# Gate and up projections of a decoder layer's feed-forward stages by seven block products instead of eight

## The chip, the cores and the metric

The kernel runs on one NeuronCore of a Trainium2 chip. The metric is device time of one execution in microseconds (us), lower is better.

## The reference

One decoder layer for a sequence of 1024 tokens of width 1024, all in float32. The two feed-forward stages are where the change is made:

```python
def _swiglu(h, w_gu, w_down):
    a, b = jnp.split(h @ w_gu, 2, axis=-1)
    return (jax.nn.silu(a) * b) @ w_down
...
        x = x + 0.5 * _swiglu(_rmsnorm(x, ffn1_norm[l]), ffn1_w_gu[l], ffn1_w_down[l])
...
        x = x + merged @ w_out[l]

        x = x + 0.5 * _swiglu(_rmsnorm(x, ffn2_norm[l]), ffn2_w_gu[l], ffn2_w_down[l])
```

`w_gu` is 1024 by 5632 (gate and up, 2816 columns each), `w_down` 2816 by 1024. Between the two stages stands a mixing block: one projection of 1024 by 5632 columns, stick-breaking attention, dilated attention, attention into 256 memory tokens, three gated branches and an output projection.

## The kernel before

**Layout and precision.** The activations stand transposed in SBUF: `xT` holds 8 tiles of 128 channels by 1024 tokens. Every large product is made of float32 values split in two parts of the type fp32r, a high part (a copy on ScalarE) and a low part (a subtraction on VectorE), and three matmuls of the parts: high by high, high by low, low by high. A weight unit is 128 by 1024 numbers (512 KB): eight blocks of 128 by 128. SyncE loads units into two buffers `raw` in a fixed order; `split_hi` (line 643, ScalarE) copies one into a slot of `w_hi`, `split_lo` (line 1020, VectorE) subtracts into `w_lo`; there are three slots. `unit_done` counts what TensorE has finished, `split_done` what is ready for it.

**A feed-forward stage.** The 2816 hidden channels are 22 tiles of 128. A tile takes a gate unit and an up unit; each is 8 blocks of channels by 3 matmuls by 2 halves of the tokens, 48 matmuls of 128x512 (`product`, line 1590). The gate goes to PSUM pair 0, the up to pair 1. VectorE multiplies the gate by the tokens' norm factor `rB` (line 1055), ScalarE applies SiLU (685), VectorE scales the up (1062), multiplies (1080), copies the high part (1082) and subtracts the low part (1086). Two tiles make a group; its `down` (line 1675) is 2 units, 96 matmuls, in 8 output tiles `m` of 12, written alternately to PSUM pairs 2 and 3, and VectorE adds each of them to `xT` (`add_tile`, 1089 and line 1096); `down` waits for `down_added` before it writes a pair again.

**Order.** The order of each engine is written out by hand. TensorE runs gate and up of the tiles 2, 3, then the down of the tiles 0, 1, and so on; five turns of a loop hold two such groups each (`ffn`, line 1734), then the last down follows. In the first stage the tiles 0 and 1 are interleaved with the projections of the memory tokens and a small product for the position bias (`toe`). At the end of the first stage the last down is interleaved on ScalarE with `gain_hi` (665, the high part of `h`) and the squares (656), on GpSimd with the sums of squares (576), and on VectorE with `gain_lo` (1032); the projection that follows on TensorE takes `h` tile by tile. The mixing block, from about 760 to 1560 us, is written out without loops.

Of the kernel before, what the change touches and what calls it, by code (L numbers as in the profile page):

```python
# [25 lines left out]
P = 128  # L26
# [16 lines left out]
BODY = 6 * GT  # L43
# [5 lines left out]
U_LOOP1 = 8  # L49
FFN_UNITS = 3 * FT  # L50
# [5 lines left out]
UNITS = U_FFN2 + FFN_UNITS  # L56
BR = (HS * HD + 2 * HD + HX * HD) // P
# [164 lines left out]
def layer(nc, x, mem, weights, gains, head_gains, rel_bias, consts, onehot, out):  # L222
    ctx = ExitStack()
    with ctx:
# [43 lines left out]
        mT_hi = at("mT_hi", AR + 48 * K, [P, DT, MEM], F32R)  # L268
# [5 lines left out]
        a_hi = at("a_hi", AR, [P, 2 * GT, S], F32R)  # L274
        a_lo = at("a_lo", AR + 16 * K, [P, 2 * GT, S], F32R)
        silu = at("silu", AR + 32 * K, [P, 2, S])
        glu = at("glu", AR + 40 * K, [P, 2, S])
# [7 lines left out]
        pr_mem = [at(f"pr_mem{i}", AR + (4 + i) * K, [P, MEM]) for i in range(3)]  # L285
# [81 lines left out]
        x0_in, x0_turned, x0_taken, h0_hi_done = sem("x0_in"), sem("x0_turned"), sem("x0_taken"), sem("h0_hi_done")  # L367
        raw0_in, w0_hi_done = sem("raw0_in"), sem("w0_hi_done")
# [17 lines left out]
        acc_hi_done, acc_split, xq_square_hi, xq_split = (sem(n) for n in ("acc_hi_done", "acc_split", "xq_square_hi", "xq_split"))  # L386
# [4 lines left out]
        tri_ready, sb_soft, sb_hi, sb_lo = sem("tri_ready"), sem("sb_soft"), sem("sb_hi"), sem("sb_lo")  # L391
# [21 lines left out]
        early_half = sem("early_half")  # L413
# [5 lines left out]

        def at_turn(k, i, step=BODY):  # L420

            return k if i is None else step * i + k
# [115 lines left out]
        def _(sp):  # L538
# [11 lines left out]
            with sp.Fori(1, UNITS // NRAW) as i:  # L550
                for r in range(NRAW):
                    sp.wait_ge(split_done, NRAW * i + r - NRAW + 1)
                    sp.dma_start(raw[:, r, :], weights[bass.ds(NRAW * i + r, 1)].rearrange("a p n -> p (a n)")
                                 ).then_inc(raw_in[r], 16)
# [12 lines left out]
        def _(pool):  # L567
# [25 lines left out]
            def xq_square_split(q):  # L593

                pool.wait_ge(xq_square, q + 1)
                pool.wait_ge(xq_square_hi, q + 1)
                nc.gpsimd.tensor_tensor(xq_sq_lo[:, (q + 1) % 2, :], xq_sq[:, (q + 1) % 2, :], xq_sq_hi[:, (q + 1) % 2, :].bitcast(F32),
                                        ALU.subtract).then_inc(xq_split, 1)
# [43 lines left out]
        def _(act):  # L642
            def split_hi(k, i=None):

                if i is None and k >= UNITS:
                    return
                act.wait_ge(raw_in[k % NRAW], 16 * (at_turn(k // NRAW, i, BODY // NRAW) + 1))
                after(act, unit_done, at_turn(k, i) - NW + 1)
                nc.scalar.activation(w_hi[:, k % NW].rearrange("p a b -> p (a b)"), raw[:, k % NRAW, :],  # L649
                                     ACT.Copy).then_inc(hi_done, 1)  # L650
# [25 lines left out]
            def ffn_tile(k, t, i=None):  # L676

                split_hi(k + AHEAD, i)
                silu_tile(t, i)
                split_hi(k + 1 + AHEAD, i)  # L680

            def silu_tile(t, i=None):

                act.wait_ge(gate_scaled, at_turn(t, i, 2 * GT) + 1)
                nc.scalar.activation(silu[:, t % 2, :], silu[:, t % 2, :], ACT.Silu).then_inc(silu_done, 1)  # L685

            def ffn(f, u0):
                t0, u1 = FT * f, u0 + 2 * GT
                if f:
                    for q in range(GT):  # L690
                        ffn_tile(u0 + 2 * q, t0 + q)
                with act.Fori(0, (NGRP - 1) // 2) as i:
                    for half in range(2):
                        k = u1 + 3 * GT * half
                        for q in range(GT):
                            ffn_tile(k + 2 * q, t0 + GT * (1 + half) + q, i)
                        for q in range(GT):
                            split_hi(k + 2 * GT + q + AHEAD, i)
                for q in range(GT - 1):
                    split_hi(u0 + FFN_UNITS - GT + q + AHEAD)  # L700

# [62 lines left out]
            for k in range(DT):  # L764
                if k == 0:
                    act.wait_ge(raw0_in, 16)
                    nc.scalar.activation(w_hi[:, 0, 0, :], raw[:, 0, 0:P], ACT.Copy).then_inc(w0_hi_done, 1)
                    act.wait_ge(x0_taken, 1)
                    nc.scalar.activation(h_hi[:, 0, 0:512], xT[:, 0, 0:512], ACT.Copy, scale=g32[:, 0, 0:1]).then_inc(h0_hi_done, 1)
# [34 lines left out]
            silu_tile(0)  # L804
            act.dma_start(oh[:], onehot).then_inc(onehot_in, 16)
            split_hi(7)
            split_hi(8)
            silu_tile(1)
            split_hi(9)
            act.wait_ge(toe_kept, 2)  # L810
            act.dma_start(toe_row[:, :], toe[:, :]).then_inc(toe_out, 16)
            ffn(0, U_LOOP1 - 2 * GT)
# [51 lines left out]
            def xq_squares(q):  # L864
# [5 lines left out]
                nc.scalar.activation(xq_sq_hi[:, (q + 1) % 2, :], x_q[:, b - 6, cols], ACT.Square).then_inc(xq_square_hi, 1)  # L870
# [133 lines left out]
            ffn(1, U_FFN2)  # L1004
# [14 lines left out]
        def _(dve):  # L1019
            def split_lo(k, i=None):  # L1020

                if i is None and k >= UNITS:
                    return
# [74 lines left out]
            def add_down(g, k, m0=0, i=None, finish=None):  # L1098
# [4 lines left out]
                for m in range(m0, DT):  # L1103
# [3 lines left out]
                    if finish:  # L1107
                        finish(m)
# [1211 lines left out]
```

## Time and profile before

| | |
|---|---|
| median of 3 runs | 2309.69 us |
| lowest and highest | 2308.91 and 2310.46 us |
| span of the profiled execution | 2307.9 us, 25807 instructions |
| TensorE busy | 2292.0 us (99%), 10616 matmuls |
| VectorE, ScalarE, GpSimd busy | 1143.3, 619.1, 142.2 us (50%, 27%, 6%) |
| chain that ended last | 95% TensorE |
| granted TensorE clock | full in every slice |
| HBM read, written | 116.42 MB, 9.87 MB |

The span runs from the first to the last instruction of the one profiled execution; the runs' median is 1.8 us above it, which is what lies around the span and the spread of executions. Matmuls are pipelined, so that the 0.39 us of a matmul's record is not what it costs in a row of them; the distance between starts is.

### The profile page before, as it was taken

The numbers are of one execution on the slowest core, as the hardware profiler recorded it, in microseconds if no ns is written. First come the engines' busy times: TensorE is split into PE (matmuls) and PEld (weight loads), VectorE is DVE, ScalarE is ACT, GpSimd is POOL, SyncE is SP. The second block draws the span as 40 slices with busy tenths as digits, with TensorE's granted clock in tenths as the row PEclk, the third lists the DMA queues.
The fourth block names the chain that finished last, engine by engine and source line by source line (L and its number), as shares of the span: only waits on it lengthen the run. The fifth ranks groups of instructions, "written<-read, shape, count | busy, mean of one in ns | idle before, by whom it ended". The sixth has DMA issues, their size and how long they took to land.

```text
span 2307.9 us, 25807 instructions
## 1 busy us (share of the span) xinstructions
PE 2292.0 (99%) x10616; PEld 1855.9 (80%) x10616; DVE 1143.3 (50%) x1107; ACT 619.1 (27%) x795; POOL 142.2 (6%) x108
## 2 busy tenths in 40 slices
PE   8999999999999999999999999999999999999999
PEld 7888888888888777777778888888888888888887
DVE  7444443434445788778535333535434434444334
ACT  6211111111112578856442111324111111111111
POOL 3000000000000412221010000011000000000000
PEclk9999999999999999999999999999999999999999
DMA  5211111111112200011122111221111111111112
GB/s 167 74 46 55 46 36 55 48 52 46 54 45 71 110 28 19 28 46 37 37 29 65 55 55 46 73 101 46 46 55 45 47 53 45 51 40 55 45 55 73
DMA packets 47567, 125.77 MB, mean 54 GB/s; under 512 B 4301, under 2 KB 20973, under 8 KB 47248
## 3 DMA queue, kind: packets, MB, share of 16 engines
q1 hardware_dynamic: 45600, 112.61, 16.1%
q10 hardware_dynamic: 912, 10.11, 1.2%
q0 software_dynamic: 992, 2.15, 0.5%
q8 instruction: 47, 0.77, 0.1%
q14 instruction: 16, 0.13, 0.0%
HBM read 116.42 MB, written 9.87 MB: 55 GB/s over the span
## 4 chain that ended last, share of the span: by engine, by line
PE 95%; DVE 3%; ACT 1%; issue 0%; DMA 0%; POOL 0%; SPq 0%; another core or an unknown queue 0%; ACTq 0%; DVEq 0%
PE ps L1588 94%; DVE h_lo L1032 1%; PE ps L2130 0%; DMA x_nat<-in_x 0%; PE ps L2065 0%; DVE h_lo L1514 0%; PE ps L2222 0%; PE ps L1836 0%; DVE xT L1096 0%; ACT sb_l L844 0%; POOL sb_l L589 0%; DVE sp_lo L1310 0%; PE ps L1989 0%; ACT sb_l L842 0%; DVE w_lo L1025 0%
## 5 line engine op out<-in xcount | busy, mean ns | idle before, releaser
L1588 PE MATMUL ps<-h_hi,w_hi 128*128 128x512 f32 x2240 | 871.6, 394 | 1.6 <-ACT h_hi L771 1.0
L1588 PE MATMUL ps<-h_lo,w_hi 128*128 128x512 f32 x2240 | 861.9, 390 | 0.6 <-DVE h_lo L1514 0.4
L1588 PE MATMUL ps<-h_hi,w_lo 128*128 128x512 f32 x2240 | 699.5, 390 | 0.0
L1588 PEld LDWEIGHTS ps<-h_hi,w_hi 128*128 128x128 f32 x2240 | 420.2, 188 | 102.2 <-issue 16.6
L1588 PEld LDWEIGHTS ps<-h_hi,w_lo 128*128 128x128 f32 x2240 | 420.6, 188 | 88.5
L1588 PEld LDWEIGHTS ps<-h_lo,w_hi 128*128 128x128 f32 x2240 | 420.4, 188 | 86.1 <-DVE h_lo L1514 1.6
L649 ACT ACTIVATE w_hi<-raw 128x1024 fp32r<-128x1024 f32 x195 | 203.3, 1052 | 793.5 <-PE ps L1588 774.4
L1025 DVE TENSOR_TENSOR w_lo<-raw,w_hi 128x1024 fp32r<-128x1024 f32 x196 | 249.4, 1280 | 157.9 <-ACT w_hi L649 147.2
L1096 DVE TENSOR_TENSOR xT<-xT,ps 128x1024 f32<-128x1024 f32 x175 | 213.2, 1218 | 175.1 <-PE ps L1588 174.8
L1588 PE MATMUL ps<-a_hi,w_hi 128*128 128x512 f32 x704 | 275.0, 391 | 0.4 <-DVE xT L1096 0.4
L1588 PE MATMUL ps<-a_lo,w_hi 128*128 128x512 f32 x704 | 273.9, 389 | 0.0
L1588 PE MATMUL ps<-a_hi,w_lo 128*128 128x512 f32 x704 | 217.1, 389 | 0.0
L1062 DVE SCALAR_TENSOR_TENSOR glu<-ps,rB 128x1024 f32<-128x1024 f32 x44 | 53.9, 1224 | 265.1 <-PE ps L1588 265.1
L1055 DVE TENSOR_TENSOR silu<-ps,rB 128x1024 f32<-128x1024 f32 x44 | 53.8, 1224 | 252.1 <-PE ps L1588 252.1
L685 ACT ACTIVATE silu<-silu 128x1024 f32<-128x1024 f32 x44 | 46.6, 1060 | 439.6 <-DVE silu L1055 439.6
L1588 PEld LDWEIGHTS ps<-a_hi,w_hi 128*128 128x128 f32 x704 | 132.1, 188 | 29.0 <-DVE xT L1096 1.9
L1588 PEld LDWEIGHTS ps<-a_hi,w_lo 128*128 128x128 f32 x704 | 132.1, 188 | 27.6
L1588 PEld LDWEIGHTS ps<-a_lo,w_hi 128*128 128x128 f32 x704 | 132.2, 188 | 27.1
L576 POOL TENSOR_TENSOR acc<-acc,sq 128x1024 f32<-128x1024 f32 x21 | 56.1, 2673 | 1080.6 <-ACT sq L656 1079.9
L1454 DVE TENSOR_TENSOR gate<-ps,rB 128x1024 f32<-128x1024 f32 x24 | 29.4, 1224 | 130.3 <-PE ps L1588 130.3
L955 ACT ACTIVATE gate<-gate 128x1024 f32<-128x1024 f32 x24 | 25.0, 1057 | 172.7 <-DVE gate L1454 172.6
L1080 DVE TENSOR_TENSOR glu<-glu,silu 128x1024 f32<-128x1024 f32 x44 | 53.9, 1225 | 4.4
(236 smaller groups left out, 1578.8 us busy)
## 6 DMA issues: line engine op xcount, KB each, us to landing
raw<-in_weights SPq DMA_DIRECT2D x195, 512.0 KB, 3.6
x_keep<-xT ACTq DMA_DIRECT2D x1, 4096.0 KB, 12.4
x_back<-x_keep ACTq DMA_DIRECT2D x1, 4096.0 KB, 13.4
x_nat<-in_x SPq DMA_DIRECT2D x7, 512.0 KB, 7.5
out<-y_nat SPq DMA_DIRECT2D x7, 512.0 KB, 3.2
toe_keep<-toe_row ACTq DMA_DIRECT2D x2, 704.0 KB, 6.5
m_nat<-in_mem SPq DMA_DIRECT2D x1, 1024.0 KB, 8.1
d_fB<-d_f_keep POOLq DMA_DIRECT2D x2, 512.0 KB, 6.8
```

Of the source, the lines that this page charges most:

```text
L576: nc.gpsimd.tensor_tensor(acc[:], acc[:], sq[:, k % 2, :], ALU.add).then_inc(acc_done, 1)
L649: nc.scalar.activation(w_hi[:, k % NW].rearrange("p a b -> p (a b)"), raw[:, k % NRAW, :], ACT.Copy).then_inc(hi_done, 1)
L685: nc.scalar.activation(silu[:, t % 2, :], silu[:, t % 2, :], ACT.Silu).then_inc(silu_done, 1)
L955: nc.scalar.activation(gate_tile(m, b), gate_tile(m, b), ACT.Sigmoid).then_inc(gate_done, 1)
L1025: nc.vector.tensor_tensor(w_lo[:, k % NW].rearrange("p a b -> p (a b)"), raw[:, k % NRAW, :], w_hi[:, k % NW].rearrange("p a b -> p (a b)" ...
L1032: nc.vector.scalar_tensor_tensor(out=h_lo[:, k, :], in0=xT[:, k, :], scalar=g32[:, gain, k:k + 1], in1=h_hi[:, k, :].bitcast(F32), op0=ALU ...
L1055: nc.vector.tensor_tensor(silu[:, t % 2, :], ps[:, 0, :], rB[:], ALU.mult).then_inc(gate_scaled, 1)
L1062: nc.vector.scalar_tensor_tensor(out=glu[:, t % 2, :], in0=ps[:, 1, :], scalar=0.5, in1=rB[:], op0=ALU.mult, op1=ALU.mult).then_inc(up_sca ...
L1080: nc.vector.tensor_tensor(glu[:, t % 2, :], glu[:, t % 2, :], silu[:, t % 2, :], ALU.mult).then_inc(glu_done, 1)
L1096: nc.vector.tensor_tensor(xT[:, m, :], xT[:, m, :], ps[:, 2 + m % 2, :], ALU.add).then_inc(down_added, 1)
L1454: nc.vector.tensor_tensor(gate_tile(m, b), ps[:, merge_pair(m, b), :], rB[:], ALU.mult).then_inc(mg_taken, 1)
L1588: return pe.matmul(o, a, b, start=start, stop=stop, skip_group_check=True)
```

## The change

It computes 18 of the 22 tiles of each stage in another way and writes both stages out without loops.

The operands of a tile are seen as blocks: the weights as 2 by 2 (gate or up, by channels 0 to 511 or 512 to 1023), the tokens' `h` as 2 by 2 (the same halves of the channels, by tokens 0 to 511 or 512 to 1023). Strassen's scheme (in Winograd's form) makes the 2 by 2 result of seven block products. A block product is 4 blocks of channels by 3 matmuls of 128x512, 12 matmuls, and sums of its operands and results are made on VectorE, ScalarE and in PSUM:

- `quadrant`, `tokens_again`, `tokens_sum` (VectorE) make once for each stage four quadrants of `h`, norm factor included, and four differences of them, eight operands in all; `tokens_hi` (ScalarE) and `tokens_lo` (VectorE) split each, 128x2048 numbers an instruction.
- `weights_sum` (VectorE) makes four sums of weight blocks for a tile, `part_hi` and `part_lo` split the seven left operands, 128x512 each, into a ring of four buffers `q_hi` and `q_lo` that takes the place of `w_hi` and `w_lo`.
- `seventh` (TensorE) runs one of the seven products, `part_done` counts them. `behind_part` copies three partial results out of PSUM on ScalarE (`seven_kept`), adds to them on VectorE (`seven_added`), and does SiLU, product and split for half of the tokens at a time.
- The down products of the groups 1 to 10 go in four parts of 24 matmuls through the same ring (`down_part`). Order: tile 4, down 1, tile 5, tile 6, down 2, ..., tile 20, down 9, tile 21, down 10.
- The tiles 0 to 3 stay plain; for the tiles 2 and 3 `by_halves` reads the quadrants in place of `h`, and down 0 stands between the two halves of tile 2's gate.
- SyncE loads the weights of the 28 chunks (18 tiles, 10 downs) of a stage as 1 MB transfers.
- Around them: at the end of the first stage `split_hi(U_SB)`, the first weights of the mixing block, stands behind the second square on ScalarE, since the ring occupies the slots until then; slots are given by `w_slot`; some semaphores of other parts are merged.

```diff
+PLAIN, SEVEN, NQ = 4, 7, 4
+TILES7 = FT - PLAIN
...
+CHUNK = []
+for _t in range(PLAIN, FT):
+    CHUNK += [("tile", _t)]
+    CHUNK += [("down", (_t - 2) // 2)] if _t % 2 == 0 else []
+CHUNK += [("down", NGRP - 1)]
...
+            def chunks(f):
+
+                for c in range(CHUNKS):
+                    if c == 0:
+                        sp.wait_ge(split_done, U_HALVES[f] + 6)
+                    elif c == 1:
+                        sp.wait_ge(unit_done, U_HALVES[f] + 6)
+                    else:
+                        sp.wait_ge(part_split, NPART * f + chunk_end(c - 2))
...
+                elif p == 1:
+                    nc.scalar.activation(a_up[s][:, T1], bank(3), ACT.Copy).then_inc(seven_kept, 1)
...
+                for n in range(NPART):
+                    if n:
+                        behind_part(f, n - 1)
+                    if n == 0:
+                        tokens_hi(f, 6)
+                    if n + 3 < NPART:
+                        part_hi(f, n + 3)
+                    if n == 0:
+                        halves_hi(f, 3)
+                    if n == 1:
+                        tokens_hi(f, 7)
...
                 act.wait_ge(down_added, DT * (NGRP - 1) + k + 1)
                 gain_hi(k, 1)
                 square(1, k)
+                if k == 1:
+                    split_hi(U_SB)
...
+            def weights_sum(f, n, p):
...
+                if p == 1:
+                    nc.vector.tensor_tensor(to, a21, a22, ALU.add).then_inc(w_summed, 1)
...
+                if p == 3:
+                    nc.vector.tensor_tensor(a_full[s][:, T1], a_full[s][:, T1], bank(3), ALU.add).then_inc(seven_added, 1)
+                elif p == 4:
+                    nc.vector.tensor_tensor(a_up[s][:, T1], a_up[s][:, T1], bank(t % 2), ALU.add).then_inc(seven_added, 1)
...
+                    nc.vector.scalar_tensor_tensor(out=a_full[s][:, T1], in0=a_up[s][:, T1], scalar=0.5, in1=a_full[s][:, T1],
+                                                   op0=ALU.mult, op1=ALU.mult).then_inc(glu_done, 1)
...
+            def seventh(f, n):
+
+                kind, t, p, c = PARTS[n]
+                i = TILES7 * f + t - PLAIN
+                to, of = (bank(2) if p == 5 else bank(3) if p in (1, 3) else bank(t % 2)), (1, 4, 5, 3, 6, 0, 7)[p]
...
+                elif p in (2, 3, 4):
+                    pe.wait_ge(seven_kept, 3 * i + p - 1)
...
+                for j in range(4):
+                    hi, lo = (w[n % NQ][:, j * P:(j + 1) * P] for w in (q_hi, q_lo))
+                    mm(to, hi, tok_hi[of][:, j, :], j == 0 and p in (0, 1, 5), False)
+                    mm(to, hi, tok_lo[of][:, j, :], False, False)
+                    last = mm(to, lo, tok_hi[of][:, j, :], False, j == 3)
+                last.then_inc(part_done, 1)
```

How the instructions of VectorE stand in the order, first for the work of one tile. Before, inside the loop (`silu` and `glu` are the gate and the up of a tile):

```order
L1055 TENSOR_TENSOR silu<-ps,rB 128x1024
L1024 REGISTER_ALU
L1025 TENSOR_TENSOR w_lo<-raw,w_hi 128x1024
L1060 REGISTER_ALU
L1062 SCALAR_TENSOR_TENSOR glu<-ps,rB 128x1024
L1078 REGISTER_ALU
L1080 TENSOR_TENSOR glu<-glu,silu 128x1024
L1082 CAST a_hi<-glu 128x1024
L1086 TENSOR_TENSOR a_lo<-glu,a_hi 128x1024
L1024 REGISTER_ALU
L1025 TENSOR_TENSOR w_lo<-raw,w_hi 128x1024
```

Now, behind the fourth product of a tile, up to the down products' additions (`a_up` and `a_full` hold up and gate, `q_lo` are low parts of the ring):

```order
L1390 TENSOR_TENSOR a_full_71<-a_full_71,ps 128x512
L1371 TENSOR_TENSOR q_lo_114<-raw_0_107,q_hi_110 128x512
L1392 TENSOR_TENSOR a_up_77<-a_up_77,ps 128x512
L1395 SCALAR_TENSOR_TENSOR a_full_71<-a_up_77,a_full_71 128x512
L1363 TENSOR_TENSOR q_lo_115<-raw_1_108,q_hi_111 128x512
L1398 TENSOR_TENSOR a_full_71<-a_full_71,ps 128x512
L1363 TENSOR_TENSOR q_lo_116<-raw_1_108,q_hi_112 128x512
L1401 SCALAR_TENSOR_TENSOR a_full_71<-ps,a_full_71 128x512
L1409 TENSOR_TENSOR a_lo_74<-a_full_71,a_hi_80 128x512
L1363 TENSOR_TENSOR q_lo_113<-raw_1_108,q_hi_109 128x512
L1409 TENSOR_TENSOR a_lo_74<-a_full_71,a_hi_80 128x512
L1314 TENSOR_TENSOR xT<-xT,ps 128x1024 x2
```

Fewer wide instructions have become many of half the width: 18 of 128x512 for one tile (the four sums of weights and some low parts stand ahead of these rows), where four of 128x1024, a cast and the splits of two units stood.

The second place is the end of the first stage on ScalarE, behind the last part of the last down (`acc` and `sq` are squares, `h_hi` the high part of `h`). Before:

```order
L649 ACTIVATE w_hi<-raw 128x1024
L813 ACT_TABLE_LOAD
L816 DMA toe_keep<-toe_row 128x1408 x2
L665 ACTIVATE h_hi<-xT,g_58 128x1024
L656 ACTIVATE acc<-xT 128x1024
L665 ACTIVATE h_hi<-xT,g_58 128x1024
```

Now:

```order
L1006 ACT_TABLE_LOAD
L1009 DMA toe_keep<-toe_row 128x1408 x2
L778 ACTIVATE h_hi<-xT,g_58 128x1024
L769 ACTIVATE acc<-xT 128x1024
L778 ACTIVATE h_hi<-xT,g_58 128x1024
L769 ACTIVATE sq<-xT 128x1024
L762 ACTIVATE w_hi<-raw 128x1024
```

The split `w_hi` of the mixing block's first weights, which stood ahead of the first `h_hi` before, is now behind the second square. On VectorE the matching `w_lo` stands now, as before, ahead of the third addition to `xT`:

```order
L1314 TENSOR_TENSOR xT<-xT,ps 128x1024 x2
L1237 SCALAR_TENSOR_TENSOR h_lo<-xT,g_58,h_hi 128x1024
L1363 TENSOR_TENSOR q_lo_114<-raw_1_108,q_hi_110 128x512
L1230 TENSOR_TENSOR w_lo<-raw,w_hi 128x1024
L1314 TENSOR_TENSOR xT<-xT,ps 128x1024
```

## Rows read from the trace of the kernel before

**Rows 1.** The page: busy time of the engines, granted clock, the chain that ended last.
```profile
PE 2292.0 (99%) x10616; PEld 1855.9 (80%) x10616; DVE 1143.3 (50%) x1107; ACT 619.1 (27%) x795; POOL 142.2 (6%) x108
...
PEclk9999999999999999999999999999999999999999
...
PE 95%; DVE 3%; ACT 1%; issue 0%; DMA 0%; POOL 0%; SPq 0%; another core or an unknown queue 0%; ACTq 0%; DVEq 0%
```

**Rows 2.** What TensorE waited for: total us, times, longest us.
```profile
PE ps L1842 <- DMA x_nat<-in_x: 4.1, 1, 4.1
PE ps L1588 <- DVE sb_a L1317: 1.2, 5, 0.3
```

**Rows 3.** VectorE in time order, second stage's loop: start us, duration us, instruction.
```profile
1893.24 1.23 DVE L1055 TENSOR_TENSOR silu<-ps,rB 128x1024 f32<-128x1024 f32 x1 [7.49 <-PE ps L1588]
...
1958.42 1.23 DVE L1055 TENSOR_TENSOR silu<-ps,rB 128x1024 f32<-128x1024 f32 x1 [7.39 <-PE ps L1588]
...
2023.80 1.22 DVE L1055 TENSOR_TENSOR silu<-ps,rB 128x1024 f32<-128x1024 f32 x1 [7.48 <-PE ps L1588]
```

**Rows 4.** VectorE in time order, mixing block, written out: gate units' results.
```profile
1357.76 1.22 DVE L1454 TENSOR_TENSOR gate<-ps,rB 128x1024 f32<-128x1024 f32 x1 [6.36 <-PE ps L1588]
1376.80 1.23 DVE L1454 TENSOR_TENSOR gate<-ps,rB 128x1024 f32<-128x1024 f32 x1 [6.16 <-PE ps L1588]
1387.68 1.22 DVE L1454 TENSOR_TENSOR gate<-ps,rB 128x1024 f32<-128x1024 f32 x1 [6.36 <-PE ps L1588]
```

**Rows 5.** Single lines: durations in ns (least, median, most), first and last start.
```profile
L1344 DVE TENSOR_TENSOR sb_qk<-pr_x,sb_qk x8: 680/682/685, 812.6 to 915.3; 128x512 fp32r<-128x512 f32 x8
...
L1338 DVE TENSOR_TENSOR pr_x<-ps,rB x10: 690/692/693, 829.2 to 1001.8; 128x512 f32<-128x512 f32 x10
...
L1096 DVE TENSOR_TENSOR xT<-xT,ps x175: 1206/1220/1223, 128.3 to 2298.9; 128x1024 f32<-128x1024 f32 x175
...
L870 ACT ACTIVATE xq_sq_hi<-x_q x4: 617/620/623, 947.3 to 984.4; 128x512 fp32r<-128x512 f32 x4
...
L649 ACT ACTIVATE w_hi<-raw x195: 1040/1045/1065, 10.4 to 2273.9; 128x1024 fp32r<-128x1024 f32 x195
```

**Rows 6.** Windows of the loops: length, busy us of PE, PEld, DVE, ACT, POOL, clock.
```profile
80.00:740.00 660.00, 660.00 (x2911) 545.15 (x2908) 283.92 (x248) 83.89 (x83) 0.00 (x0) 1.00 0.16 49
```

**Rows 7.** The page: DMA issues, KB each, us from issue to landing.
```profile
raw<-in_weights SPq DMA_DIRECT2D x195, 512.0 KB, 3.6
...
m_nat<-in_mem SPq DMA_DIRECT2D x1, 1024.0 KB, 8.1
```

**Rows 8.** VectorE in time order, beginning of the first stage.
```profile
60.52 0.43 DVE L1172 SCALAR_TENSOR_TENSOR pr_mem<-ps,pr_mem 128x256 f32<-128x256 f32 x1 [3.97 <-ACT pr_mem L743]
...
72.03 0.42 DVE L1183 COPY mv<-ps 128x256 f32<-128x256 f32 x1 [1.25 <-PE ps L1827]
78.88 1.22 DVE L1062 SCALAR_TENSOR_TENSOR glu<-ps,rB 128x1024 f32<-128x1024 f32 x1 [6.43 <-PE ps L1588]
81.34 1.21 DVE L1267 COPY toe<-ps 2x1024 f32<-2x1024 f32 x1 [1.24 <-PE ps L1588]
```

**Rows 9.** End of the first stage in time order: ScalarE, VectorE, TensorE, GpSimd.
```profile
743.01 1.04 ACT L656 ACTIVATE sq<-xT 128x1024 f32<-128x1024 f32 x1
...
742.40 1.22 DVE L1025 TENSOR_TENSOR w_lo<-raw,w_hi 128x1024 fp32r<-128x1024 f32 x1
743.54 1.21 DVE L1096 TENSOR_TENSOR xT<-xT,ps 128x1024 f32<-128x1024 f32 x1
...
747.83 0.61 PE L1588 MATMUL ps<-a_hi,w_lo 128*128 128x512 f32 x2
748.81 0.50 PE L1588 MATMUL ps<-a_hi,w_hi 128*128 128x512 f32 x1 [0.37 <-DVE xT L1096]
...
744.14 2.41 POOL L576 TENSOR_TENSOR acc<-acc,sq 128x1024 f32<-128x1024 f32 x1 [704.16 <-ACT sq L656]
```

**Rows 10.** VectorE in time order beside a busy GpSimd.
```profile
1558.25 2.57 DVE L1025 TENSOR_TENSOR w_lo<-raw,w_hi 128x1024 fp32r<-128x1024 f32 x1 [2.07 <-ACT w_hi L649]
```

More of the change, by code:

```diff
@@ L412, in layer @@
         y_turned, y_ready, y_out = sem("y_turned"), sem("y_ready"), sem("y_out")
-        early_half = sem("early_half")
+        tok_made, tok_hi_done, tok_split = (sem(f"tok_{n}") for n in ("made", "hi_done", "split"))
+        w_summed, part_hi_done, part_split, part_done = (sem(n) for n in ("w_summed", "part_hi_done", "part_split", "part_done"))
+        seven_kept, seven_added = sem("seven_kept"), sem("seven_added")
         def after(eng, s, value):
@@ L674, in rstd, with silu_tile @@
                 nc.scalar.activation(sq[:, 0, :], rB[:], ACT.Square).then_inc(rstd_done, 1)
[L676 to L700, printed above, removed]
+            def silu_tile(f, t):
+                act.wait_ge(gate_scaled, 2 * f + t + 1)
+                nc.scalar.activation(a_full[t][:], a_full[t][:], ACT.Silu).then_inc(silu_done, 1)
@@ new lines, in glu_product, with quadrant @@
+                nc.vector.tensor_tensor(a_lo[t][:], a_full[t][:], a_hi[t][:].bitcast(F32), ALU.subtract).then_inc(a_ready, 1)
+            def quadrant(f, to, half_d, half_t, j0=0, j1=4):
+                for j in range(j0, j1):
+                    k = 4 * half_d + j
+                    nc.vector.scalar_tensor_tensor(out=tok[to][:, j, :], in0=xT[:, k, BOTH[half_t]], scalar=g32[:, 2 * f, k:k + 1],
+                                                   in1=rB[:, BOTH[half_t]], op0=ALU.mult, op1=ALU.mult).then_inc(tok_made, 1)
@@ new lines, in by_halves @@
+            def by_halves(f, part, k, half):
+                for half_d in (1, 0):
+                    i = ((1, 0), (2, 3))[half][half_d]
+                    pe.wait_ge(tok_split, 8 * f + i + 1)
+                    for j in range(4):
+                        hi, lo = (w[:, w_slot(k), 4 * half_d + j, :] for w in (w_hi, w_lo))
+                        mm(bank(2 * part + half), hi, tok_hi[i][:, j, :], half_d == 1 and j == 0, False)
+                        mm(bank(2 * part + half), hi, tok_lo[i][:, j, :], False, False)
+                        last = mm(bank(2 * part + half), lo, tok_hi[i][:, j, :], False, half_d == 0 and j == 3)
+                return last
@@ new lines, in down_mm @@
+            def down_mm(m, q, hi, lo, t, first, final, halves=BOTH, within=None):
+                for cols in halves:
+                    if within and cols == T1:
+                        within()
+                    mm(ps[:, 2 + m % 2, cols], hi, a_hi[t % 3][:, cols], first, False)
+                    mm(ps[:, 2 + m % 2, cols], hi, a_lo[t % 3][:, cols], False, False)
+                for cols in halves:
+                    last = mm(ps[:, 2 + m % 2, cols], lo, a_hi[t % 3][:, cols], False, final)
+                return last
@@ L2288, in weight_units @@
         units += gates[m] + [branches[m]]
[L2289 removed]
+    plain, chunks = swiglu_units(f2_gu, f2_down)
+    units += column_units(w_out, range(DT)) + plain + chunks
     return np.ascontiguousarray(np.stack(units))
```

694 lines of the change are left out of this document (485 added, 209 removed).

## The prediction, made before the run

> **What bounds the kernel now.** I read the page first: TensorE is busy 99% of the span, the chain that ended last is 95% TensorE, and the granted clock is full in every slice (2.4 GHz, the higher of its two levels) [rows 1]. Then its waits: the largest is the first load of x, 4.1 us once, and the next entry is 1.2 us in five pieces [rows 2]. So time goes down only by fewer or cheaper matmuls, and goes up by any new wait of TensorE. For the price of a matmul I do not take its record of 0.39 us, since the records overlap, but the distance of equal places in the loop: from the first to the third result of a group's first gate it is 2023.80 - 1893.24 = 130.56 us [rows 3], two groups of 288 matmuls, so 0.2267 us each. The single groups take 65.18 and 65.38 us, one with the loop's end and one without; together they are exactly 576 matmuls, so the turn of the loop costs nothing that shows, and writing the loops out gains nothing.
>
> **The matmuls.** Before, a tile takes 2 x 48 = 96 matmuls of 128x512, after it 7 x 12 = 84. The type (fp32r), the width and the weight load for each matmul stay. 18 tiles x 2 stages x 12 = 432 matmuls go, and the down products and tiles 0 to 3 keep theirs. 432 x 0.2267 = **97.9 us less**.
> The row says 0.2267 us, with a weight load for each matmul. The Trainium skill has another figure: "TensorE: Matmul & The Clock Gate", section "Back-to-back issue gap", gives about 131 ns as the sustained spacing at width 512 in a stream of loads and matmuls; by it the gain would be 432 x 0.131 = 57 us. The trace contradicts it, and the row decides.
>
> **The boundaries.** Each product now begins behind three semaphore waits, and there are 252 product boundaries and 80 of down parts in both stages. The nearest rows are in the mixing block, which is written out as well: from 1376.80 to 1387.68 one gate unit of 48 matmuls, 10.88 us, and from 1357.76 to 1376.80 three branch products and a gate unit, 84 matmuls behind four product boundaries with one to three waits, 19.04 us [rows 4]. Both are 0.2267 us a matmul, so a wait that is already granted costs nothing. I take 0 for each boundary. A wait that is granted late costs what it is late and about 0.2 us more: from the pair at 747.83 to the next matmul it is 0.98 us in place of 0.45, 0.53 more for a wait of 0.37 [rows 9].
>
> **VectorE in the steady state.** Per tile it makes 4 sums of weights, 7 low parts, 3 additions, 2 products and 2 low parts of the result, 18 instructions of 128x512 as the order counts them; per down 4 low parts of that width and 8 additions of 128x1024. The 512-wide ones take 0.68 us from SBUF and 0.69 from PSUM, the additions 1.22 [rows 5]. A group is then 40 x 0.69 + 8 x 1.22 = 37.4 us of VectorE in 264 x 0.2267 = 59.8 us of TensorE, 62% against 43% before [rows 6]. ScalarE: 7 high parts, 3 copies, 2 SiLU, 2 high parts of the result per tile, 4 per down, 32 x 0.62 = 19.8 us [rows 5]. A product lasts 12 x 0.2267 = 2.72 us, and the tightest handoff gives one product's time: the product p1 ends, ScalarE copies it out (0.6 us) during p2, and p3 writes over it. A ring entry is split by VectorE after the product three ahead of it began and needs at most 0.69 + 0.69 + 0.68 us of queue before it, with 5.4 us to go. Both fit. Transfers: 1 MB landed in 8.1 us, beside others, and 512 KB in 3.6 [rows 7]; a chunk is asked for when the one two before it is split, seven products or 19 us ahead. **Cost 0.**
> A rule speaks against this part: the Trainium skill, "Advanced Engine Details and Errata", section "The Read-Write Bubble", tells to use large tiles, since each instruction of VectorE and ScalarE exposes the memory's latency. The rows bear the size out (two of 512 take 1.38 us, one of 1024 1.22), and halving the width thus adds 40 x 0.08 = 3.2 us to a group, inside VectorE's free 22 us.
>
> **The start of each stage.** Eight operands have to be made of the tokens. No row is 2048 wide; from 0.69 at 512 and 1.22 at 1024 [rows 5] I extrapolate 2.28 us, back to back 2.2, and for ScalarE 1.9. In the first stage VectorE sits idle for 3.97 us before 60.52, which takes the first quadrant (4 x 0.64 = 2.6 us), and idles again between 72.5 and 78.88 [rows 8], which takes a low part, the second quadrant and a weight split. Its second low part ends about 81.7, the scaling of the up slips from 78.88 to 81.7, and the low part of tile 1 is ready near 89.0. TensorE, which ends the small product at 81.3, then has 24 matmuls by halves (to 86.6) and 12 of down 0 (to 89.4): no wait. But then VectorE makes the third quadrant before it adds the first output tile, at 92.7, which output tile 2 wants at 92.1: 0.7 + 0.2, **0.9 us**. In the second stage no small product is in the way and this falls within 0.1 us. In both, when the plain tiles end, ScalarE has the seventh split of the tokens, two high parts, tile 3's high part, the copy of p0, and the last split of the tokens (2 us) queued ahead of the copy of p1, and so ends that copy 8.7 us after the plain tiles' end, where p3 wants it after 3 x 2.72 = 8.2: 0.6 + 0.2, **0.8 us in each, 1.6**. Bounds for the start together: 0 (the extrapolated widths are too long) and 7 us (VectorE 1 us later at each of the four places in each stage).
>
> **The end of the first stage.** Here a step is moved. Before, VectorE split the next weights at 742.40 and added output tile 2 at 743.54, done at 744.75, ahead of the 745.4 at which TensorE wanted its pair [rows 9]. Now the high part comes behind the second square, which ended at 744.05; it takes 1.05, so the low part starts at 745.1, and GpSimd's first sum starts at 744.14 as well. Alone the low part takes 1.2 us, beside GpSimd it took 2.57 [rows 10]. Tile 2 is added at 747.5 to 748.9: TensorE waits 2.1 to 3.5, I take the middle and 0.2 for the late wait, 3.0. The last tile's low part comes about 0.3 us late for the last down. Before had the late wait of 0.5 us there [rows 9], which these replace. Net **2.8 us** (2.1 to 3.5). In the second stage's end the split is not there: 0.
>
> **Sum.** 2307.9 - 97.9 + 0.9 + 1.6 + 2.8 = 2215.3 us of span. The median of the runs stands 1.8 above the span shown, so 2217.1, rounded to **2217 us**. About 0.2% (4.6 us) is what a measurement of this kernel can tell from no change.
>
> **The rivals.**
> *Late handoffs in every tile* (0.13). The chain PSUM, ScalarE copy, VectorE addition, SiLU, product has to keep up with 2.72 us. For it: four-deep ring, strict order on two engines, three waits per product. Against: 62% and 33% load. Once in a tile, 0.2 for a late wait and 0.4 lateness: 36 x 0.6 = 22 us, 2239.
> *Boundaries cost after all* (0.05). If each of the 332 took 0.11 us, half of what a late wait adds: 37 us, 2253. Against it stand the two distances in the mixing block [rows 4].
> *VectorE becomes the bound, slower than before* (0.03). It decides once 40 x d + 8 x 1.22 exceeds 59.8 us, d = 1.25 us for a 512-wide instruction; before's 65.3 us for a group is passed at d = 1.39. The only row near is the 2.57 us of a 1024-wide one beside GpSimd [rows 10], 1.29 for half. Such slow instructions with a per-instruction rest, 1.5 us each, would make a group 69.8 us; with 9 groups in each of two stages that is 10.0 us more than forecast, 18 x 10.0 = 180 us, 2397. Against it: GpSimd is idle from 80 to 740 us [rows 6] and the change gives it nothing there.
> *The granted clock falls* (0.01). Short waits of TensorE in every product could let it fall to 1.2 GHz; then the two stages' 36 x 19 = 684 us of products would double, far above before, near 2900. Against: the clock stays full in the mixing block, where TensorE waits most [rows 1]. The Trainium skill, "TensorE: Matmul & The Clock Gate", section "A second HAM failure mode: psum-queue depth-cycling", describes such a fall from small idles between matmul groups; no row here shows it.
> *The change does not save what it says*: the order shows 432 fewer matmuls, the loop's turns counted, so only their price could differ.
>
> **How the numbers follow.** The forecast has 0.78; its own range goes by the bounds: with the start at 0 and the end at 2.1 the sum gives 2213.9, and 4 us less for the spread of executions and for small waits of before that go, 2210; with the start at 7 and the end at 3.5 it gives 2222.3, and 4 us more for as many late waits again that I overlook, 2226. The range that should hold 8 of 10 reaches to the first rival: 2210 to 2240. Faster by over 0.2%: 0.78 + 0.13 + 0.05 = 0.96, taken as 0.95; slower 0.04; within 0.2%: 0.01.
>
> **What would show it.** Right: TensorE's starts of equal products of two tiles 59.8 us a group apart; VectorE near 60% busy there; 10184 matmuls; waits of TensorE on lines of the two stages of some 5 us in sum, the longest near the end of the first on an addition to xT. Wrong: a wait on `seven_kept`, `part_split` or `seven_added` repeated 36 times; 512-wide instructions above 0.8 us; a clock below full in the loops' place.

## The result, and the profile after the change

The changed kernel takes **2219.24 us** in the median, the kernel before beside it 2310.07; the ratio is 0.9605, with a 95% interval of 0.959 to 0.962. Measured a second time (e11) it takes 2217.30 (2216.93 to 2220.80), ratio 0.9604. The forecast was 2217, the range 2210 to 2240. One execution here took 9163.63 us and one in e5 4972.23, for no reason that was found; the two medians on record count them, the ratios do not, and without them the medians are 2218.72 here and 2214.94 in e5. Where a difference from the changed kernel is given below, it is from **2218.0 us**, the median of its other eight executions in both measurements (2216.93 to 2220.80).

The page of the changed kernel, the lines that answer to [rows 1]:

```profile
span 2215.4 us, 25422 instructions
...
PE 2196.4 (99%) x10184; PEld 1775.5 (80%) x10184; DVE 1354.8 (61%) x1591; ACT 844.4 (38%) x1251; POOL 139.8 (6%) x108
...
PEclk9999999999999999999999999999999999999999
...
PE 96%; DVE 2%; ACT 1%; issue 1%; DMA 0%; POOL 0%; SPq 0%; ACTq 0%; DVEq 0%
```

TensorE is still at 99% and still the chain; only its work is less. The engine that filled up is VectorE, and its windows say how far: length, busy time of PE, PEld, DVE, ACT and POOL, granted clock, between equal places of two groups and over most of the first stage (before: [rows 6]):

```profile
319.22:379.03 59.81, 59.81 (x265) 49.53 (x264) 35.52 (x48) 18.81 (x32) 0.00 (x0) 1.00 0.15 54
120.00:680.00 560.00, 559.61 (x2469) 463.08 (x2469) 338.28 (x439) 178.14 (x293) 0.00 (x0) 1.00 0.15 53
```

What TensorE waited for (before: [rows 2]), the entries that are new or grew. Two lines of the stages are among them, the addition to xT and an "issue":

```profile
PE ps L1931 <- DVE xT L1314: 3.1, 1, 3.1
PE ps L1931 <- issue: 0.8, 2, 0.4
```

**The end of the first stage**, in time order, answers to [rows 9]. VectorE:

```profile
697.05 2.49 DVE L1230 TENSOR_TENSOR w_lo<-raw,w_hi 128x1024 fp32r<-128x1024 f32 x1 [2.02 <-ACT w_hi L762]
699.46 1.21 DVE L1314 TENSOR_TENSOR xT<-xT,ps 128x1024 f32<-128x1024 f32 x1
```

TensorE there, and the window that belongs to it:

```profile
700.82 0.76 PE L1931 MATMUL ps<-a_hi,q_hi 128*128 128x512 f32 x1 [3.07 <-DVE xT L1314]
701.38 0.63 PE L1931 MATMUL ps<-a_lo,q_hi 128*128 128x512 f32 x1
701.81 0.63 PE L1931 MATMUL ps<-a_hi,q_hi 128*128 128x512 f32 x1
702.23 0.63 PE L1931 MATMUL ps<-a_lo,q_hi 128*128 128x512 f32 x1
702.66 1.05 PE L1931 MATMUL ps<-a_hi,q_lo 128*128 128x512 f32 x2
703.51 0.48 PE L1931 MATMUL ps<-a_hi,q_hi 128*128 128x512 f32 x1
```

```profile
700.80:703.50 2.70, 2.68 (x6) 2.13 (x7) 2.20 (x2) 2.47 (x3) 0.62 (x1) 0.50 0.45 170
```

The predicted chain is there link by link: the high part of the next weights comes behind the second square, VectorE waits 2.02 us for it, its low part takes 2.49 us while GpSimd works, and only then is output tile 2 added, 3.07 us late. Behind the wait stands something that was not predicted: matmuls start 0.43 us apart in place of 0.23, at a granted clock of 0.50, the lower of its two levels (1.2 GHz). The page's line of the clock, 55 us to a digit, does not show it; the window does.

### The profile page after: what moved, and what is told of

Its sections match the earlier page's. It is cut to its first block, busy times and chain, and to the rows that moved or that the text cites. A ratio compares the mean times of both kernels' runs of the same rounds, so it can differ in the third digit from the quotient of the medians.

```text
span 2215.4 us, 25422 instructions
## 1 busy us (share of the span) xinstructions
PE 2196.4 (99%) x10184; PEld 1775.5 (80%) x10184; DVE 1354.8 (61%) x1591; ACT 844.4 (38%) x1251; POOL 139.8 (6%) x108
## 4 chain that ended last, share of the span: by engine, by line
PE 96%; DVE 2%; ACT 1%; issue 1%; DMA 0%; POOL 0%; SPq 0%; ACTq 0%; DVEq 0%
PE ps L1931 94%; PE ps L2527 1%; DMA x_nat<-in_x 0%; PE ps L2462 0%; DVE h_lo L1843 0%; PE ps L2619 0%; PE ps L2234 0%; DVE w_lo L1230 0%; ACT w_hi L762 0%; ACT sb_l L1039 0%; POOL sb_l L698 0%; DVE sp_lo L1639 0%; PE ps L2386 0%; ACT sb_l L1037 0%; DVE sb_a L1646 0%
## 5 line engine op out<-in xcount | busy, mean ns | idle before, releaser
L1931 PE MATMUL ps<-tok_hi,q_hi 128*128 128x512 f32 x1008 | 392.3, 389 | 0.8 <-issue 0.8
L1931 PE MATMUL ps<-tok_hi,q_lo 128*128 128x512 f32 x1008 | 392.1, 389 | 0.0
L1931 PE MATMUL ps<-tok_lo,q_hi 128*128 128x512 f32 x1008 | 392.1, 389 | 0.0
L1931 PE MATMUL ps<-h_hi,w_hi 128*128 128x512 f32 x960 | 373.4, 400 | 1.7 <-ACT h_hi L962 1.1
L1931 PE MATMUL ps<-h_lo,w_hi 128*128 128x512 f32 x960 | 363.8, 391 | 0.6 <-DVE h_lo L1843 0.6
L1931 PE MATMUL ps<-h_hi,w_lo 128*128 128x512 f32 x960 | 305.5, 390 | 0.0
L1931 PE MATMUL ps<-a_hi,q_hi 128*128 128x512 f32 x640 | 250.7, 392 | 3.1 <-DVE xT L1314 3.1
L1931 PE MATMUL ps<-a_lo,q_hi 128*128 128x512 f32 x640 | 249.5, 390 | 0.0
L1931 PEld LDWEIGHTS ps<-h_hi,w_lo 128*128 128x128 f32 x960 | 180.3, 188 | 38.7
L1931 PEld LDWEIGHTS ps<-h_lo,w_hi 128*128 128x128 f32 x960 | 180.1, 188 | 36.0 <-DVE h_lo L1843 1.7
```

The source lines that it names most:

```text
L1931: return pe.matmul(o, a, b, start=start, stop=stop, skip_group_check=True)
```

## The experiments

**Is the time all TensorE's?** e1 gives back the removed product, e2 multiplies the waits, e10 leaves out a further product's worth of each tile, so that its output is no longer the layer's. All three edit the loop of `seventh`.

```diff
-                for j in range(4):
+                for j in (range(4) if p else (0, 1, 2, 3, 0, 1, 2, 3)):     # e1
+                    pe.wait_ge(part_split, NPART * f + n + 1)               # e2, inside the old loop
+                for j in ((0, 3) if p in (2, 4) else range(4)):             # e10
```

> The first of the seven products of every tile is computed twice, the second pass starting its sum anew: 96 matmuls per tile as before the change, with every other instruction, wait and the missing loops of the changed kernel. Theory (TensorE alone sets the time, one matmul is 0.2267 us, everything else the change added lies beside it but for some 5 us at the ends): 36 x 12 x 0.2267 = 97.9 us more than the changed kernel, 2219.2 + 97.9 = 2317.1, that is 7 above the kernel before. Rival (the products wait in each tile on a handoff, which longer first products would cover): part of the added work is hidden, below 2310. Rival (a matmul of this stream costs less than 0.2267, with another loss of the same size beside it): the rise is below 90 us.

Measured: 2315.22 us (2312.93 to 2316.01), ratio to before 1.0024 (1.0014 to 1.0033). 97.2 us more than the changed kernel, where 97.9 was expected, and 6.0 above the kernel before. Both rivals fall for the tiles at large: nothing repeated in every tile was waiting. On a small scale the first holds at the start of the stages, for the two waits of 0.40 and 0.39 us of the changed kernel's trace (at p3, the fourth product of a tile; see e6) are gone, covered by the longer first product. In their place this trace has a wait of 1.68 us on the mixing block's weights, which comes up again in e11.

> Every product of a tile waits before each of its four steps of three matmuls once more on the semaphore of its weights, which is already granted: 4 x 252 = 1008 waits more in both stages. Theory (a granted wait costs nothing on TensorE): 2219, within 1 us of the changed kernel. Rival (a boundary costs about 0.11 us even if granted): 1008 x 0.11 = 111 us more, 2330; at 0.02 us each it would still be 20 us more.

Measured: 2217.51 us, ratio 0.9602 (0.9586 to 0.9618). That is 0.5 us less than the changed kernel, inside its scatter: 1008 waits cost nothing that shows, and at 0.02 us each they would have cost 20. The run prices waits that are already granted. That a boundary as a whole is free is shown by the distance of two groups, 59.84 us for 264 matmuls with all their boundaries, 0.2267 us each.

> Left out: the middle two of the four steps of the third and the fifth product of every tile, 12 matmuls, so that a tile has 72; every other instruction and wait stays. It asks whether TensorE would still be the bound of one saving more of the same size. Theory (TensorE alone sets the time, VectorE's load goes from 60 to 66%): 97.9 us less than the changed kernel, 2121, or up to 10 more where a shortened product of 1.36 us makes the handoff behind it late. Rival (the handoffs have no more to give): above 2150.

Measured: 2123.83 us, ratio 0.9197 (0.9183 to 0.9211), 94.2 less than the changed kernel. Equal additions of two tiles a group apart, in e10:

```profile
322.84 0.69 DVE L1390 TENSOR_TENSOR a_full<-a_full,ps 128x512 f32<-128x512 f32 x1 [2.24 <-PE ps L1931]
...
377.24 0.69 DVE L1390 TENSOR_TENSOR a_full<-a_full,ps 128x512 f32<-128x512 f32 x1 [2.24 <-PE ps L1931]
```

54.40 us = 240 x 0.2267: the steady state would give the whole of one saving more. Of the 97.9 us 3.7 are missing. Some 2.7 of them are at the start of the stages, where p3's wait grew from 0.40 to 1.75 us, twice, and 1 is a longer wait on `d_st` in the mixing block (1.9 in place of 0.8).

**How much room does VectorE have?** The repeats go in front of the four sums of weights and of the low parts of p0, p5 and p6; `N` is 1 in e9, 2 in e3, 3 in e4.

```diff
+            def more(*args):
+                for _ in range(N):
+                    nc.vector.tensor_tensor(*args).then_inc(again, 1)
+                    repeats[0] += 1
+                    dve.wait_ge(again, repeats[0])
...
+                    more(to, a21, a22, ALU.add)
                     nc.vector.tensor_tensor(to, a21, a22, ALU.add).then_inc(w_summed, 1)
```

> Seven 512-wide instructions of VectorE per tile (the four sums of weights and the low parts of the three unsummed weights) are each made three times, each repeat waiting for the one before it. VectorE's load is 36.1 us of a group's 59.8 now; 28 instructions of 0.69 more give 55.4 to 58.2 us, 93 to 97%. Theory (VectorE has slack and its handoffs have several us of queue): little change in the mean but some late handoffs where the repeats lie in bursts, 0 to 1 us a tile, 2219 to 2255. Rival (the handoffs are tight already, each late one costs its whole lateness): a product stretched by the repeats in front of the additions, 1.4 us a tile and more, above 2270.

> The same seven instructions four times. VectorE's load is 36.1 + 42 x 0.69 = 65.1 us a group without the time between a repeat and its wait, 69.3 with 0.1 us for each. Theory (VectorE becomes the bound when its load passes 59.8 us a group): a group takes 65.1 to 69.3, 18 groups x (5.3 to 9.5) = 95 to 171 us more, 2314 to 2390, and TensorE waits in every tile. Rival (something else sets the pace of the group, VectorE's work is hidden behind it): below 2280.

> The same seven instructions of VectorE per tile twice. Three times cost 5.3 us a group of 59.8 (65.1 between equal waits), 28 instructions more; four times cost 8.0 us more for the next 14, 0.57 each. Theory (a hinge: below some load nothing is late, above it each further instruction counts in full; 5.3 / 0.57 = 9 of the 28 are beyond it): 14 more lie inside the slack, 2219 to 2225. Rival (each added instruction costs from the first one on, 0.19 us): 18 x 14 x 0.19 = 48 us, 2267.

Measured: twice 2223.85 us (2223.26 to 2224.34), three times 2313.32 (2311.58 to 2315.55), four times 2452.95 (2447.70 to 2453.65). Twice came out as its theory said, within 2219 to 2225. Three times was expected within 2219 to 2255 by the theory, and came out with its rival. Four times was expected at 2314 to 2390 and lies 63 us above that, so the rule behind it, that VectorE binds once its load passes the 59.8 us of TensorE's work, is wrong too: it binds earlier. The windows of e3 and e4:

```profile
120.00:680.00 560.00, 526.81 (x2267) 423.38 (x2266) 468.74 (x638) 160.46 (x269) 0.00 (x0) 1.00 0.14 49
```

```profile
120.00:680.00 560.00, 491.68 (x2020) 390.31 (x2020) 487.57 (x672) 143.80 (x241) 0.00 (x0) 0.96 0.12 43
```

VectorE sets the pace at 84% busy (468.74 of 560), and reaches only 87% when pressed further. In e4 part of the time is TensorE's clock, 0.96 in this window. TensorE's waits in one group of e3, all there are between equal places 65.10 us apart:

```profile
319.09 0.47 PE L1945 MATMUL ps<-a_hi,q_hi 128*128 128x512 f32 x1 [1.21 <-DVE xT L1315]
344.06 0.50 PE L1945 MATMUL ps<-tok_hi,q_hi 128*128 128x512 f32 x1 [0.25 <-DVE q_lo L1385]
347.51 0.50 PE L1945 MATMUL ps<-tok_hi,q_hi 128*128 128x512 f32 x1 [0.43 <-DVE q_lo L1385]
352.05 0.47 PE L1945 MATMUL ps<-tok_hi,q_hi 128*128 128x512 f32 x1 [1.51 <-DVE q_lo L1385]
355.50 0.47 PE L1945 MATMUL ps<-tok_hi,q_hi 128*128 128x512 f32 x1 [0.45 <-issue]
384.19 0.47 PE L1945 MATMUL ps<-a_hi,q_hi 128*128 128x512 f32 x1 [1.21 <-DVE xT L1315]
```

Five late waits in a group, 3.85 us, and what a late wait adds each time; 18 x (65.10 - 59.84) = 94.7 us, measured 95.3. And while it set the pace VectorE still stood idle, over two groups 9.8 us ahead of additions, for results of TensorE (its group of that line, busy us, mean ns, idle us before):

```profile
L1315 DVE TENSOR_TENSOR xT<-xT,ps 128x1024 f32<-128x1024 f32 x16 | 19.3, 1218 | 9.8 <-PE ps L1945 9.8
```

In these two groups VectorE was idle for 21.6 us, 16.5 of them ahead of instructions that take a result of TensorE. It works through a written order, so it stops at a result that is not there yet, and splits that TensorE will want stand queued behind; the two engines wait for each other in turn, and neither is full. The 84% belongs to this order and to repeats that stand in bursts, each behind a wait for the one before it; no run spreads them out. With everything twice a group takes 60.03 us (equal additions at 321.18 and 381.21), 0.19 more than without, 3.4 us in the kernel. The rest of the 5.8 us is at the starts, where p3 waits 1.84 and 1.85 us in place of 0.40 and 0.39. So 14 instructions more are nearly free, the next 14 cost 5.07 us a group, 0.36 each, and the 14 after them 7.8, 0.55 each.

**The two places that were predicted to wait.** Both get their own edit (e5, e6), e7 has both, e8 moves the other end of the same handoff.

```diff
-                        if f == 0 and n == NPART - 3:    # VectorE, ffn: split_lo(U_SB)
+                        if f == 0 and n == NPART - 2:    # e5, e7
...
-                    if n == 1:                           # ScalarE, ffn: tokens_hi(f, 7)
+                    if n == 2:                           # e6, e7
...
-                if k == 1:                               # ScalarE, behind ffn(0): split_hi(U_SB)
+                if k == 0:                               # e8
```

> At the end of the first stage VectorE splits the next stage's first weights one part later, behind the addition of output tile 3 in place of ahead of that of output tile 2. Theory (the wait of 3.07 us is the queue in front of that addition, and the half clock behind it, some 1.3 us, is its consequence): the wait goes down to 0.4 us or less, no slice there shows the clock at half, and the kernel is 3.5 to 4.5 us faster than the changed one, 2214.7 to 2215.7. Rival (the half clock comes from elsewhere, e.g. the change of stage): only 2.5 to 3.0 us, and matmuls 0.43 us apart stay near 700 us. Rival (the split is late next and the projection behind the stage waits for it): less than 1 us.

Measured: 2214.94 us (2215.21 on record, see the result), ratio 0.9593 (0.9580 to 0.9605). That is 3.1 us less, under the 3.5 to 4.5 expected, and the time alone does not tell the theory from its first rival; but its five executions (2214.76 to 2215.57) all lie below the changed kernel's eight, and the trace decides for the theory. The wait has gone and the clock stays full where the matmuls had been 0.43 us apart. In its place three short waits of 0.3 to 0.4 us stand on later additions; with some 0.2 us for each late wait they take back 1.7 of the 4.6 us lost there (worked out in the next section), which fits the 3.1:

```profile
PE ps L1931 <- DVE xT L1314: 1.1, 3, 0.4
```

```profile
700.80:702.60 1.80, 1.50 (x7) 1.11 (x7) 1.80 (x2) 1.35 (x2) 1.54 (x1) 1.00 0.00 0
```

> ScalarE makes the high part of the next stage's first weights after the first square in place of the second; VectorE's order stays. The high part then starts at 693.9 in place of 695.9, VectorE's low part at about 695.0, alone 1.2 us long, and output tile 2 is added at 696.2 to 697.4, ahead of the 697.75 at which TensorE wants its pair; but output tile 1's high part and square come 1 us later each. Theory (wait is only the queue): TensorE's wait of 3.07 us goes to 0.3 or less and the clock stays full, 3.3 to 4.4 us faster than the changed kernel. Rival (GpSimd's sum or the later squares slow what follows): a gain of 1 to 2 us.

Measured: 2215.59 us, ratio 0.9595 (0.9582 to 0.9607), 2.4 us less, between the 3.3 to 4.4 of the theory and the 1 to 2 of its rival. Half of each holds. Output tile 2 is added 2.1 us earlier than in the changed kernel, not 3.3, and TensorE still waits 1.04 us for it; a second wait of 1.15 us comes in on output tile 3's addition, which stands behind a low part that runs beside GpSimd's sum, as the rival said:

```profile
698.49 3.16 DVE L1237 SCALAR_TENSOR_TENSOR h_lo<-xT,g,h_hi 128x1024 fp32r<-128x1024 f32 x1
```

```profile
698.18 2.39 POOL L685 TENSOR_TENSOR acc<-acc,sq 128x1024 f32<-128x1024 f32 x1 [658.31 <-ACT sq L769]
```

The clock stays full behind both waits.

> ScalarE makes the high part of the eighth sum of tokens after the copy of the second product and the high part of the sixth weights, not ahead of that copy. Theory (p3 waits 0.40 and 0.39 us for that copy, 0.55 us with what a late wait adds): both gaps go and nothing else becomes late, 1.1 us less in all, 2218.1. Rival (VectorE's low part of it comes later and holds back the addition of the fourth product): no gain or a loss of up to 2 us.

Measured: 2218.04 us (2215.27 to 2220.70), ratio 0.9606 (0.9593 to 0.9618). The executions scatter over 5 us and their median is that of the changed kernel's eight, so the time settles nothing. The trace does: in the changed kernel TensorE waits twice at p3,

```profile
155.74 0.47 PE L1931 MATMUL ps<-tok_hi,q_hi 128*128 128x512 f32 x1 [0.40 <-issue]
...
1650.83 0.47 PE L1931 MATMUL ps<-tok_hi,q_hi 128*128 128x512 f32 x1 [0.39 <-issue]
```

and in e6, as in e7, there is no wait from 140 to 172 us nor from 1640 to 1670.

> Both moves together. Theory (they touch different places): the gains add, 4.6 to 5.6 us less than the changed kernel, 2213.6 to 2214.6. Rival: one of them is not there.

Measured: **2213.51 us** (2213.26 to 2214.39), ratio 0.9586 (0.9574 to 0.9599): 1.4 us less than e5's 2214.94, and 4.5 less than the changed kernel, just short of the 4.6 to 5.6 expected. Its slowest execution is faster than the fastest of e5 and of the changed kernel. It is the fastest kernel of the study that computes the whole layer.

**The scatter.** The changed kernel's executions lie within 3.9 us, those of e7 within 1.1.

> The changed kernel itself, unchanged, beside the others of this call. It asks two things: whether the 3.07 us wait at the end of the first stage is there again (theory: yes, it is the order of VectorE's queue, 3.0 to 3.1 us), and whether TensorE's granted clock falls to half behind it (it did in the changed kernel's trace and not in that of the run with the later split of the tokens, with the same wait). If the clock's fall is a matter of the single execution, times scatter over 1 to 2 us around 2219, where the kernels without the wait kept within 1.1.

Measured: 2217.30 us. The wait of 3.07 us is there again, and the clock fell again. The profiled execution took 2219.41 us and has a wait that the first one did not have, on the next weights' low part. In e11 VectorE and GpSimd:

```profile
723.99 3.40 DVE L1230 TENSOR_TENSOR w_lo<-raw,w_hi 128x1024 fp32r<-128x1024 f32 x1
```

```profile
722.95 3.35 POOL L688 TENSOR_TENSOR acc_lo<-acc,acc_hi 128x1024 fp32r<-128x1024 f32 x1 [1.17 <-ACT acc_hi L774]
```

```profile
727.43 0.74 PE L1931 MATMUL ps<-h_hi,w_lo 128*128 128x512 f32 x2 [1.67 <-DVE w_lo L1230]
```

and in the first trace, 2217.16 us, with the starts the other way round:

```profile
723.56 1.21 DVE L1230 TENSOR_TENSOR w_lo<-raw,w_hi 128x1024 fp32r<-128x1024 f32 x1
```

```profile
723.73 3.30 POOL L688 TENSOR_TENSOR acc_lo<-acc,acc_hi 128x1024 fp32r<-128x1024 f32 x1 [1.18 <-ACT acc_hi L774]
```

e12 fixes that order:

```diff
                     pool.wait_ge(acc_hi_done, r)
+                    if r == 1:
+                        pool.wait_ge(split_done, U_SB + AHEAD)
```

> The changed kernel, where GpSimd's last step on the first stage's squares (acc_lo) also waits until VectorE has split the second weights of the mixing block. In the traces so far this split took 1.21 us where it began 0.16 to 0.17 us ahead of acc_lo, and 3.40 where acc_lo began 1.0 us ahead of it, and then TensorE waited 1.67 us. Theory (this order, left to chance, makes the executions of the changed kernel scatter over 3.9 us): VectorE's split takes 1.2 us, no wait on it, and the times keep within 1.5 us, median 2217. TensorE's wait of 3.07 us and the half clock behind it are not touched. Rival (the scatter comes from the clock's fall): the times still spread over 3 us or more. Price, if the order was right anyway: GpSimd starts some 1 us later, 0 to 0.5 us.

Measured: 2218.94 us (2218.61 to 2219.70), ratio 0.9606 (0.9593 to 0.9619). VectorE's split took 1.21 us and nothing waited for it; the times keep within 1.1 us in place of 3.9, though the clock still fell in the profiled one. The median did not come down to 2217.

That the order is the source of most of the scatter is not shown by this, on 5 executions against 8, for the record has a second source beside it. Each execution's mean granted clock is known: of the changed kernel's eight the fastest has 1.000, the two slowest have 0.998, the five between them 0.999, and e1's ten fall apart in the same way, three at 1.000 from 2312.93 to 2313.11 us and seven at 0.999 from 2315.01 to 2316.01. None of e12's five has 0.998. Nor are the two sources apart: the split took 3.4 us in five traces (e1, e2, e3, e4, e11), in all of which the clock had fallen at the end of the first stage, and in none of the five in which it stayed full there (e5 to e9). The fall shifts what follows and so can turn the order over. How much of the scatter each makes was not separated.

e12's trace has a new wait of 0.23 us of TensorE on acc_lo, the price named, and one of 1.3 us on `d_st` in the mixing block, which e10's has too (1.4) and the changed kernel's has not. What sets that one off was not tried.

## Why the prediction was right, step by step

- **The matmuls, -97.9 us: right.** Equal additions a group apart stand at 319.22 and 379.06, 59.84 us = 264 x 0.2267, against (65.18 + 65.38)/2 = 65.28 before. 18 x 5.44 = 97.9. e1 gives it back with 97 us and e10 takes it once more in the steady state. The other price considered, 57 us by the spacing in the Trainium skill, "TensorE: Matmul & The Clock Gate", section "Back-to-back issue gap", is contradicted by all three.
- **The boundaries, 0: right.** e2 shows it for granted waits, the 59.84 us for the boundaries as a whole. Loops written out, seven products, new waits and new order come together to e1's 6.0 us over the kernel before; e1's trace has no wait at p3, and the start's 0.3, the end's 4.1 and the 1.68 us wait on the mixing block's weights make 6.1.
- **VectorE, cost 0: right, for a reason that was too weak.** The load was overestimated a little, 37.4 us a group against 35.52: the durations of neighbours overlap, 319.22 to 319.83 for one of 0.69 us. What failed is the rival's deciding point, that VectorE becomes the bound "once 40 x d + 8 x 1.22 exceeds 59.8 us". By e3 it binds at 84% busy, 54.3 us of work in a group of 65.1. Of the "free 22 us" some 10 can be used: e9 takes 9.3 of them nearly for nothing (44.77 us busy in a group of 60.03), e3's next 9.6 cost 5. None of the signs named for the rivals is in the changed kernel's trace: no wait is repeated 36 times, the 512-wide instructions take 0.69 us, and the clock is full over the steady state.
- **The start, 0.9 and 1.6 us: places right, sizes too large.** VectorE's third quadrant took 2.73 us from 88.15, and the first addition started at 90.98; TensorE's start gaps there sum to 0.3 us in place of 0.9 (92.26 after a pair that began at 91.62, and 0.11 behind it). p3's wait was 0.40 and 0.39 us, with what a late wait adds 0.55 each, 1.1 in place of 1.6. e6 shows the named cause, the last split of the tokens ahead of the copy of p1. The upper bound of 7 us for the start names eight places at 1 us, which would be 8; nothing came near either.
- **The end, net 2.8 us: mechanism right, and one term missing.** Predicted were 3.0 for the late addition with its late wait, less the 0.5 of before. From 697.13 to 703.51 TensorE starts 8 matmuls, 8 x 0.2267 = 1.8 us of work in 6.38, so the loss is 4.6: 3.07 of wait, some 0.3 that follow a late wait, and 1.2 at half clock (five starts 0.43 us apart in place of 0.23, and a longer first one). Net 4.1. The text held a fall of the clock possible in every product and priced it there, but not behind the one long wait it forecast itself.
- **The sum.** 2307.9 - 97.9 + 0.3 + 1.1 + 4.1 = 2215.5, the span is 2215.4. That the forecast's 2215.3 comes within 0.1 us of it is luck: starts 1.1 us too high stand against an end 1.3 too low. The 1.8 us from span to time hold for each execution, but the profiled one (2217.16 us) is the second fastest of the eight; the median of the eight stands 2.6 us above its span.

## What to carry to other kernels

Where one engine is the chain at 99%, taking work from it pays by the measured distance of equal places, not by record durations, and granted waits cost nothing. The engine that takes over the work can set the pace well before 100%, here at 84%, because its written order also waits; load it artificially in two or three steps to see where that is before giving it more. And what is left to gain then lies at the seams, in which instruction stands ahead of which: two instructions moved in their engines' orders brought 4.5 us.

## What the runs showed of the hardware that was not expected

**The clock behind one long wait.** TensorE, busy for hundreds of microseconds before, waited 3.07 us once at the end of the first stage, in ten traces of kernels that keep this order. In eight the granted clock was half (1.2 GHz) for some microseconds of the work behind it; in e6 and e9 it stayed full. In e9 it fell elsewhere, behind a wait of 1.85 us at 1654.41:

```profile
1654.41 0.47 PE L1945 MATMUL ps<-tok_hi,q_hi 128*128 128x512 f32 x1 [1.85 <-issue]
...
1655.22 0.63 PE L1945 MATMUL ps<-tok_hi,q_hi 128*128 128x512 f32 x1
1655.65 0.63 PE L1945 MATMUL ps<-tok_lo,q_hi 128*128 128x512 f32 x1
...
1658.59 0.40 PE L1945 MATMUL ps<-tok_hi,q_lo 128*128 128x512 f32 x1
```

```profile
1656.00:1658.00 2.00, 2.00 (x6) 1.53 (x5) 1.97 (x3) 0.00 (x0) 0.00 (x0) 0.50 0.00 0
```

and did not behind the equal one of 1.84 us at 157.26. So the same wait of 3.07 us cost 4.6 in the changed kernel's trace and 3.3 in e6's, where the clock stayed full (from 696.98 to 702.10 us it starts 8 matmuls, 1.8 us of work in 5.1); what decides between the two, no run here shows. e4, which waits in every tile, has a mean clock of 0.98.

**VectorE beside GpSimd.** The same 1024-wide split takes 1.21 us if it starts 0.17 us ahead of GpSimd's instruction and 3.40 if it starts 1.04 behind. In e5 a gain-and-subtract that otherwise takes 1.28 us takes 3.38 beside it:

```profile
696.71 3.38 DVE L1237 SCALAR_TENSOR_TENSOR h_lo<-xT,g,h_hi 128x1024 fp32r<-128x1024 f32 x1
```

```profile
696.59 2.41 POOL L685 TENSOR_TENSOR acc<-acc,sq 128x1024 f32<-128x1024 f32 x1 [656.48 <-ACT sq L769]
```

The end says more than the length. Where such an instruction of VectorE, both inputs in SBUF, began while one of GpSimd was running, it ended 1.08 to 1.09 us after GpSimd's had ended: so in all five pairs shown or named here (697.05 and 709.97 in the changed kernel, and those of e5, e8 and e11). That is nearly its whole length alone, as if it had stood still until then. Where VectorE's began first, it took its 1.21 us, and GpSimd's `acc_lo` 3.30 in place of the 2.39 of e12. The additions to `xT`, which read one input from PSUM, keep their 1.21 us beside a running GpSimd (e5, 700.01 beside 699.52). What such a pair costs is thus settled by which of the two begins first and by how much of the first is left, and a shift of under a microsecond upstream turned it over between two traces of the same kernel.
